# Four score and forget-gate matmuls per attention unit: two heads together, or head by head

## The chip, the cores and the metric

The kernel runs on one core of one Trainium2 chip. The metric is the device time of one execution in microseconds (us); lower is better. PE is TensorE, DVE is VectorE, ACT is ScalarE, POOL is GpSimd, SP issues the weight transfers. The kernel is written instruction by instruction: every engine has its own program, and semaphores tie the programs together.

## The reference

Two transformer blocks stand one behind the other, on 256 tokens of width 1024, all in float32. The change lies in the second block, in its forgetting attention (8 heads of width 64, computed in two query blocks of 128 tokens):

```python
q = rms_norm_2(heads(q), q_norm); k = rms_norm_2(heads(k), k_norm)      # B, H=8, S=256, hd=64
cum = jnp.cumsum(log_f, axis=-1)                                        # B, H, S
s = jnp.einsum('bhqd,bhkd->bhqk', q_i, k) * scale
s = s + c_i[..., :, None] - cum[..., None, :]                           # c_i: cum at the queries
s = jnp.where(pos_k[None, :] <= pos_q[:, None], s, -jnp.inf)
pr = jax.nn.softmax(s, axis=-1)
o = jnp.einsum('bhqk,bhkd->bhqd', pr, v)
```

Around it stand: rms norm and an input projection (w_in), an RWKV-7 mixer on the other half of the width, sigmoid gates, two projections (rwkv_proj, fox_proj), an output projection (w_out), and feed-forward parts before and after.

## The kernel before

All weights come in chunks of 1 MB (128 partitions x 2048 floats). SP loads a chunk into one of three `w_raw` buffers; ACT copies it to `w_hi` in the rounded format fp32r (L1316); DVE takes `w_lo` = `w_raw` - `w_hi` (L1602). PE multiplies in three parts, high x high, low x high, high x low (L1987, L1988, L1989): one chunk by columns is 48 matmuls of 128x256. PE's order is written out by hand, and so is that of ACT and DVE; nothing is scheduled by a planner.

The change is in `f_scores(it)`, a closure in `pe_mixer`. It computes the scores of one attention unit: `it` runs from 0 to 7, `t = it // 2` picks a pair of heads, `i = it % 2` the query block. With i = 0 the keys are 128 wide, with i = 1 they are 256 wide. The two heads of a pair lie in one tile of 128 partitions: head 0 in partitions 0 to 63, head 1 in partitions 64 to 127 (`head(v, h, ...)` takes that slice). So a score matmul contracts over 64 partitions. The forget term is added by a second matmul into the same bank: its left side is one column of the identity spread over 128 columns, its right side the cumulated forget gates, and both lie in partitions 32 to 39 (`32:32 + NH`, NH = 8), for either head. Head 0 goes to PSUM bank 4, head 1 to bank 5. These operands are plain float32, and the trace shows two matmul records for each such matmul of the program. The last of the four increments `f_scores`.

What follows a block: DVE adds the query's term and the causal mask (L1082) and takes the row maximum (L1088); ACT takes the exponential (L819); DVE normalizes (L1100); PE turns the probabilities (L695); ACT copies them out of PSUM (L830); PE multiplies by v (L706); ACT and DVE write the result as high and low part (L834, L1118).

The order on PE: block 0; the gate columns of chunk B_GA+3 with block 1 in their middle (after 18 of 48 matmuls); then for each unit `it`: a chunk of matmuls (gate columns for it < 5, a chunk of rwkv_proj by rows for it = 5 and 6), the transposes of unit `it`, `f_scores(it + 2)`, and the product with v of unit `it`. Blocks 2 to 7 so stand between L695 and L706. DVE's order in unit `it`: the gate columns out of PSUM (L1639), the scores of unit it+2, the normalization of unit it+1, the low part of the output of unit `it` (L1118), and the w_lo of a later chunk (L1602). The chunk of unit 5 waits until DVE has read the gate columns of unit 4 (L1639).

Of the kernel before, what the change touches and what calls it, by code (L numbers as in the profile page):

```python
# [14 lines left out]
P = 128  # L15
# [21 lines left out]
NH = HALF // HD  # L37
# [51 lines left out]
def block_pair(nc, inp, out, scratch, shifted):  # L89

    ctx = ExitStack()
    with ctx:
        S = Signals(nc, ctx)

        def sb(name, shape, dt=F32):
            return ctx.enter_context(nc.sbuf_tensor(name, shape, dt))

        bank = [ctx.enter_context(nc.psum_tensor(f"bank{b}", [P, 512], F32)) for b in range(8)]
# [7 lines left out]
        ident, ones, head_ones = sb("ident", [P, P]), sb("ones", [P, P]), sb("head_ones", [P, P])  # L106
# [7 lines left out]
        def region(at, *shape):  # L114
            n = int(np.prod(shape))
            assert at + n <= ARENA
            v = arena[:, at:at + n]
            if len(shape) == 2:
                v = v.rearrange("p (a b) -> p a b", a=shape[0])
            if len(shape) == 3:  # L120
                v = v.rearrange("p (a b c) -> p a b c", a=shape[0], b=shape[1])
            return v
# [210 lines left out]
        forget = region(18440, T)  # L333
# [6 lines left out]
        fq, fk = region(16384, HT, T), region(17408, HT, T)  # L340
# [92 lines left out]
        def head(v, h, *rest):  # L433
            return v[(slice(HD * h, HD * (h + 1)), *rest)]


        def pe_mixer(told, pe, state, by_columns, by_tokens, by_rows, rows_to_tokens, turn_late_half, spread):
# [42 lines left out]
            for t in range(HT):  # L480
                mm = pe.matmul(bank[6 + t // 2][:, t % 2 * T:t % 2 * T + T], lora_w[0:32, 0, t * P:(t + 1) * P],
                               lora_act[0:32, 0, :], start=True, stop=True)
            mm.then_inc(S["decay_in"], told.one("decay_in"))
            for t in range(HT):
                mm = pe.matmul(bank[4 + t // 2][:, t % 2 * T:t % 2 * T + T], lora_w[32:64, 0, t * P:(t + 1) * P],
                               lora_act[32:64, 0, :], start=True, stop=True)
# [7 lines left out]
            for t in range(HT):  # L494
                o = bank[6 + t // 2][:, t % 2 * T:t % 2 * T + T]
                pe.matmul(o, lora_w[64:128, 0, t * P:(t + 1) * P], lora_act[64:128, 0, :], start=True, stop=False)
                mm = pe.matmul(o, lora_w[0:32, 1, t * P:(t + 1) * P], lora_act[0:32, 1, :], start=False, stop=True)
# [8 lines left out]
            for tt in range(TT):  # L506
                mm = pe.matmul(bank[3][:, 256 + tt * NH:256 + (tt + 1) * NH], forget[32:32 + NH, tt * P:(tt + 1) * P],
                               ident[32:32 + NH, 32:32 + NH], start=True, stop=True)
# [5 lines left out]
            for t in range(HT):  # L514
                mm = pe.matmul(bank[6 + t // 2][:, t % 2 * T:t % 2 * T + T], head_ones[:, :], early[:, t, :],
                               start=True, stop=True)
# [5 lines left out]
            for c in range(NCH):  # L522
                if c > 1:
                    pe.wait_ge(S["masked"], 2 * (c - 1))
                for src, b in ((b_dec, 4 + 2 * (c % 2)), (k_dec, 5 + 2 * (c % 2))):
                    for t in range(HT):
                        for h in range(2):
                            mm = pe.matmul(head(bank[b], h, slice(t * P, (t + 1) * P)),  # L528
                                           head(src, h, t, slice(c * CHUNK, (c + 1) * CHUNK)),
                                           head(ar, h, c * HT + t), start=True, stop=True)  # L530
# [10 lines left out]
            for u in range(NCH * HT):  # L541
                for h in range(2):
                    mm = pe.matmul(head(bank[6 + u // 8], h, slice(u % 8 * CHUNK, u % 8 * CHUNK + CHUNK)),
                                   head(xt_inv, h, u), head(ident, h, slice(HD * h, HD * (h + 1))),
                                   start=True, stop=True)
# [54 lines left out]
            for c in range(NCH):  # L600
                def each(fn):
                    for t in range(HT):
                        for h in range(2):
                            mm = fn(t, h, c * HT + t)
                    return mm

                def cell(b, t, h):
                    return head(bank[b], h, slice(t * CHUNK, (t + 1) * CHUNK))

                def mul(o, left, right, start, stop):  # L610
                    return pe.matmul(o, left, right, start=start, stop=stop, skip_group_check=True)  # L611

                def decayed(k, u, h):
                    return head(ar, h, u, slice(k * CHUNK, (k + 1) * CHUNK))

                pe.wait_ge(S["xt_added"], 2 * LEVELS)
                if c > 0:
                    pe.wait_ge(S["w_copied"], c)
                mm = each(lambda t, h, u: mul(cell(4, t, h), head(m_k, h, u, slice(0, CHUNK)), head(v_tok, h, u),
                                              t == 0, not c and t == HT - 1))  # L620
                if c:
                    pe.wait_ge(S["state"], c)
                    mm = each(lambda t, h, u: mul(cell(4, t, h), decayed(0, u, h), head(state_t, h, t), False,
                                                  t == HT - 1))
# [22 lines left out]
            for t in range(HT):  # L647
                mm = pe.matmul(bank[4 + t // 2][:, t % 2 * T:t % 2 * T + T], head_ones[:, :], y_t[:, t, :],
                               start=True, stop=True)
# [13 lines left out]
            def f_scores(it):  # L663

                t, i = divmod(it, TT)
                w = P * (i + 1)
                if it == 0:
                    pe.wait_ge(S["normed_by_head"], 6)
                else:
                    pe.wait_ge(S["f_scores_read"], 2 * it)  # L670
                for h in range(2):

                    pe.matmul(bank[4 + h][:, 0:w], head(fq, h, t, slice(i * P, (i + 1) * P)),
                              head(fk, h, t, slice(0, w)), start=True, stop=False)
                for h in range(2):
                    c = 32 + 2 * t + h
                    mm = pe.matmul(bank[4 + h][:, 0:w], ident[32:32 + NH, c:c + 1].to_broadcast([NH, P]),
                                   forget[32:32 + NH, 0:w], start=False, stop=True)
                mm.then_inc(S["f_scores"], told.one("f_scores"))

            f_scores(0)
            for it in range(FUNITS):
                t, i = divmod(it, TT)
                if it < 5:
                    columns(B_GA + 3 + it, midway=(lambda: f_scores(1)) if it == 0 else None)
                elif it < 7:

                    r = it - 5
                    pe.wait_ge(S["y_lo"], 1)
                    for b, c in enumerate(all_read(B_RP)):  # L690
                        pe.wait_ge(S[f"bank{b}_read"], c)
                    by_rows(B_RP + r, (B_RP + r) % RING, 0, Y_hi, Y_lo, 2 * r, r == 0, r == 1)
                pe.wait_ge(S["f_probs"], it + 1)
                for b in range(2 * (i + 1)):
                    mm = pe.transpose(bank[6][:, b * P:(b + 1) * P], fs_t[:, it % 2, b * P:(b + 1) * P], ident[:])  # L695
                mm.then_inc(S["f_probs_turned"], told.one("f_probs_turned"))
                if it + 2 < FUNITS:
                    f_scores(it + 2)
                pe.wait_ge(S["fpT_ready"], it + 1)
                if it > 0:  # L700
                    pe.wait_ge(S["f_out_lo"], it)
                for h in range(2):
                    for kb in range(i + 1):
                        b = h * (i + 1) + kb
                        c = (2 * t + h) * HD
                        mm = pe.matmul(head(bank[7], h, slice(0, P)), fv[:, kb, c:c + HD],  # L706
                                       fpT[:, b * P:(b + 1) * P], start=kb == 0, stop=kb == i)
                mm.then_inc(S["f_pv_done"], told.one("f_pv_done"))
# [1568 lines left out]
```

## Time and profile before

| | |
|---|---|
| median of 3 runs | 1203.66 us (1203.29 to 1204.83) |
| profiled execution, its time | 1203.29 us |
| its span | 1201.5 us |
| PE busy | 1144.5 us, 95% |
| DVE busy | 771.0 us, 64% |
| ACT busy | 557.2 us, 46% |
| granted TensorE clock, mean | 0.981 |
| first and last score block (L673) | start 895.17 and 947.57 us |

The span runs from the first to the last instruction that the profile shows; the execution's time is 1.8 us longer. A matmul's record has a modelled end, and records overlap, so the cost of a group of matmuls is best read from its start to the start of what comes next. A merged row of the time order shows the start of the first record, the stretch that the group covers, and after it how many records there are. In brackets stands how long the engine had been idle, and what ended that.

### The profile page before, as it was taken

To read this page: it belongs to the slowest core of one execution; us is meant where nothing else is said; L and a number is where in the kernel's file an instruction comes from. 1 tells how busy PE (TensorE), PEld (TensorE's weight loads), DVE (VectorE), ACT (ScalarE), POOL (GpSimd) and SP (SyncE) were. 2 spreads that over 40 slices of the span, in tenths; PEclk is the share of its full clock that TensorE was granted. 3 is DMA by queue.
4 is the path that set the end of the run, shared out by engine and by line. 5 is a ranking of instruction groups with operands and counts; after the bars stand their busy time and mean duration, and the time that the engine had idled before them with its cause. 6 is when DMAs were issued, how large, how long until landed. Compare 5 with 4: busy or idle time off the path is not lost.

```text
span 1201.5 us, 22075 instructions
## 1 busy us (share of the span) xinstructions
PE 1144.5 (95%) x9584; PEld 1078.9 (90%) x9584; DVE 771.0 (64%) x1042; ACT 557.2 (46%) x660; POOL 150.0 (12%) x112
## 2 busy tenths in 40 slices
PE   7999999989999999899999979999899889999997
PEld 6999999988899999799999968989898778999996
DVE  4888976747686777756455656963257655645554
ACT  6333445473764455654433454422334446434433
POOL 5888760000000000000000000012000000000000
PEclk9999999999999999999999988999999989999999
DMA  8586553344365555555556524323033433565651
GB/s 255 179 290 199 176 175 106 116 161 173 109 208 193 183 201 175 174 175 166 185 176 208 184 97 140 106 75 104 3 106 105 141 106 124 193 213 188 201 163 56
DMA packets 144315, 188.94 MB, mean 157 GB/s; under 512 B 4448, under 2 KB 128921, under 8 KB 144237
## 3 DMA queue, kind: packets, MB, share of 16 engines
q1 hardware_dynamic: 142941, 184.28, 46.3%
q0 software_dynamic: 1104, 3.49, 0.9%
q8 instruction: 58, 0.95, 0.3%
q14 instruction: 20, 0.16, 0.0%
q10 hardware_dynamic: 192, 0.05, 0.0%
HBM read 186.74 MB, written 2.64 MB: 158 GB/s over the span
## 4 chain that ended last, share of the span: by engine, by line
PE 84%; DVE 8%; ACT 5%; issue 2%; ACTq 0%; POOL 0%; DVEq 0%; POOLq 0%
PE bank L1987 19%; PE bank L1988 19%; PE bank L1989 19%; PE bank L2097 5%; PE bank L2098 5%; PE bank L2099 5%; PE bank L551 2%; DVE w_lo L1602 2%; ACT w_hi L1316 2%; PE bank L611 1%; DVE bank L1819 1%; PE bank L2224 1%; ACT sq L1330 1%; DVE x L1676 1%; PE bank L528 1%
## 5 line engine op out<-in xcount | busy, mean ns | idle before, releaser
L1987 PE MATMUL bank<-X_hi,w_hi 128*128 128x256 f32 x1840 | 527.2, 287 | 3.3 <-DVE w_lo L1775 2.9
L1988 PE MATMUL bank<-X_lo,w_hi 128*128 128x256 f32 x1840 | 523.6, 285 | 0.0
L1989 PE MATMUL bank<-X_hi,w_lo 128*128 128x256 f32 x1840 | 523.5, 285 | 0.0
L1316 ACT ACTIVATE w_hi<-w_raw 128x2048 fp32r<-128x2048 f32 x171 | 326.2, 1909 | 176.1 <-PE bank L1989 134.3
L1602 DVE TENSOR_TENSOR w_lo<-w_raw,w_hi 128x2048 fp32r<-128x2048 f32 x146 | 333.7, 2286 | 84.3 <-ACT w_hi L1316 84.0
L1987 PEld LDWEIGHTS bank<-X_hi,w_hi 128*128 128x128 f32 x1840 | 356.1, 194 | 8.6 <-issue 6.8
L1988 PEld LDWEIGHTS bank<-X_lo,w_hi 128*128 128x128 f32 x1840 | 356.2, 194 | 1.2
L1989 PEld LDWEIGHTS bank<-X_hi,w_lo 128*128 128x128 f32 x1840 | 356.0, 193 | 0.0
L1714 DVE TENSOR_TENSOR arena<-bank,rstd 128x512 f32<-128x512 f32 x66 | 45.6, 691 | 185.1 <-PE bank L1989 179.6
L1268 POOL TENSOR_TENSOR w_lo<-w_raw,w_hi 128x2048 fp32r<-128x2048 f32 x24 | 111.3, 4646 | 32.5 <-ACT w_hi L1316 32.4
L2097 PE MATMUL bank<-w_hi,Y_hi 128*128 128x512 f32 x264 | 103.3, 391 | 1.2 <-DVE Y_lo L1742 1.2
L2098 PE MATMUL bank<-w_hi,Y_lo 128*128 128x512 f32 x264 | 103.1, 390 | 0.0
L2099 PE MATMUL bank<-w_lo,Y_hi 128*128 128x512 f32 x264 | 102.7, 389 | 0.0
L1819 DVE SCALAR_TENSOR_TENSOR bank<-arena,par,bank 128x256 f32<-128x256 f32 x232 | 93.2, 484 | 0.6
L1297 POOL TENSOR_TENSOR arena<-arena,levels 128x512 f32<-128x512 f32 x10 | 12.8, 1282 | 592.6 <-DVE arena L1012 559.2
L2097 PEld LDWEIGHTS bank<-w_hi,Y_hi 128*128 128x128 f32 x264 | 49.7, 188 | 11.1 <-DVE Y_lo L1742 1.6
L2099 PEld LDWEIGHTS bank<-w_lo,Y_hi 128*128 128x128 f32 x264 | 49.6, 188 | 10.6
L2098 PEld LDWEIGHTS bank<-w_hi,Y_lo 128*128 128x128 f32 x264 | 49.7, 188 | 9.1
L1427 ACT ACTIVATE arena<-arena,par 128x256 f32<-128x256 f32 x44 | 24.1, 595 | 69.5 <-DVE arena L1714 69.5
L1436 ACT ACTIVATE arena<-arena 128x512 f32<-128x512 f32 x22 | 13.9, 633 | 84.1 <-DVE arena L1714 84.1
L1639 DVE TENSOR_TENSOR arena<-bank,rstd 128x512 f32<-128x512 f32 x43 | 29.6, 689 | 31.9 <-PE bank L1989 29.4
L1450 ACT ACTIVATE Y_hi<-arena 128x512 fp32r<-128x512 f32 x33 | 20.9, 632 | 44.0 <-DVE arena L1735 44.0
(285 smaller groups left out, 1291.9 us busy)
## 6 DMA issues: line engine op xcount, KB each, us to landing
w_raw<-in_ffn_w_dram SPq DMA_DIRECT2D x66, 1024.0 KB, 5.2
w_raw<-in_w_in_dram SPq DMA_DIRECT2D x53, 1024.0 KB, 5.1
w_raw<-in_w_up_dram SPq DMA_DIRECT2D x22, 1024.0 KB, 5.0
w_raw<-in_w_down_dram SPq DMA_DIRECT2D x11, 1024.0 KB, 4.9
w_raw<-in_w_out_dram SPq DMA_DIRECT2D x8, 1024.0 KB, 4.8
w_raw<-in_conv_pw_w_dram SPq DMA_DIRECT2D x4, 1024.0 KB, 4.9
w_raw<-in_w_attn_out_dram SPq DMA_DIRECT2D x2, 1024.0 KB, 5.1
w_raw<-in_rwkv_proj_dram SPq DMA_DIRECT2D x2, 1024.0 KB, 4.9
```

The source lines that it names most:

```text
L1268: g.tensor_tensor(w_lo[n % RING][:, :], raw[n % RING][:, :], w_hi[n % RING][:, :].bitcast(F32), ALU.subtract).then_inc(S["w_lo_pool"], tol ...
L1316: a.activation(w_hi[slot][:, :], raw[slot][:, :], ACT.Copy).then_inc(S["w_hi"], told.one("w_hi"))
L1602: v.tensor_tensor(w_lo[slot][:, :], raw[slot][:, :], w_hi[slot][:, :].bitcast(F32), ALU.subtract).then_inc(S["w_lo"], told.one("w_lo"))
L1639: v.tensor_tensor(dst, pairs(b), over(rstd[:], 2), ALU.mult).then_inc(S[f"bank{b}_read"], 1)
L1714: v.tensor_tensor(u_t[:, side].rearrange("p (m t) -> p m t", m=2), pairs(2 * (i % 2) + side), over(rstd[:], 2), ALU.mult).then_inc(S[name] ...
L1819: v.scalar_tensor_tensor(out=conv[:, t, :] if k == CONV_W - 1 else part, in0=src, scalar=w, in1=part, op0=ALU.mult, op1=ALU.add).then_inc( ...
L1987: pe.matmul(o, wh, xh, start=start, stop=False, skip_group_check=True)
L1988: pe.matmul(o, wh, xl, start=False, stop=False, skip_group_check=True)
L1989: return pe.matmul(o, wl, xh, start=False, stop=stop, skip_group_check=True)
L2097: pe.matmul(o, yh, wh, start=first and k == 0, stop=False, skip_group_check=True)
L2098: pe.matmul(o, yl, wh, start=False, stop=False, skip_group_check=True)
L2099: mm = pe.matmul(o, yh, wl, start=False, stop=last, skip_group_check=True)
```

## The change

The loop over the two heads with the two score matmuls, and the second loop with the two forget matmuls, become one loop: score and forget of head 0, then score and forget of head 1. The matmuls themselves, their banks, their start and stop flags, the waits ahead of them and the one signal behind them are the same.

```diff
                 for h in range(2):
 
-                    pe.matmul(bank[4 + h][:, 0:w], head(fq, h, t, slice(i * P, (i + 1) * P)),
-                              head(fk, h, t, slice(0, w)), start=True, stop=False)
-                for h in range(2):
+                    o = bank[4 + h][:, 0:w]
                     c = 32 + 2 * t + h
-                    mm = pe.matmul(bank[4 + h][:, 0:w], ident[32:32 + NH, c:c + 1].to_broadcast([NH, P]),
-                                   forget[32:32 + NH, 0:w], start=False, stop=True)
+                    pe.matmul(o, head(fq, h, t, slice(i * P, (i + 1) * P)), head(fk, h, t, slice(0, w)),
+                              start=True, stop=False)
+                    mm = pe.matmul(o, ident[32:32 + NH, c:c + 1].to_broadcast([NH, P]), forget[32:32 + NH, 0:w],
+                                   start=False, stop=True)
                 mm.then_inc(S["f_scores"], told.one("f_scores"))
```

On PE, block 3 (256 keys wide), between the transposes of unit 1 and the product with v. L673 and L675 are the score matmul before and now, L677 the forget matmul; `arena` holds queries, keys and gates, `ident` the identity; the number behind `bank` is the PSUM bank:

```order
 L1989 MATMUL bank1<-X_hi,w_lo1 128x256
 L695 MATMUL bank6<-ident,arena 128x128 x4
-L673 MATMUL bank4<-arena 128x256
-L673 MATMUL bank5<-arena 128x256
+L675 MATMUL bank4<-arena 128x256
 L677 MATMUL bank4<-arena,ident 128x256
+L675 MATMUL bank5<-arena 128x256
 L677 MATMUL bank5<-arena,ident 128x256
 L706 MATMUL bank7<-arena 64x128 x4
```

The score of bank 5 moved behind the forget matmul of bank 4. Block 4 (128 keys wide), in the same place of unit 2:

```order
 L1989 MATMUL bank2<-X_hi,w_lo2 128x256
 L695 MATMUL bank6<-ident,arena 128x128 x2
-L673 MATMUL bank4<-arena 128x128
-L673 MATMUL bank5<-arena 128x128
+L675 MATMUL bank4<-arena 128x128
 L677 MATMUL bank4<-arena,ident 128x128
+L675 MATMUL bank5<-arena 128x128
 L677 MATMUL bank5<-arena,ident 128x128
 L706 MATMUL bank7<-arena 64x128 x2
```

The same move; all eight blocks have it. DVE, ACT, POOL and SP keep their order in every row.

## Rows read from the trace of the kernel before

**Rows 1.** The page: busy us (share of the span) xinstructions of each engine.
```profile
PE 1144.5 (95%) x9584; PEld 1078.9 (90%) x9584; DVE 771.0 (64%) x1042; ACT 557.2 (46%) x660; POOL 150.0 (12%) x112
```
**Rows 2.** PE in order of time, block 2: start us, us, engine line operation, rows*columns, records.
```profile
905.76 0.49 PE L673 MATMUL bank<-arena 64*128 64x128 f32 x4
906.18 0.71 PE L677 MATMUL bank<-arena,ident 8*128 8x128 f32 x4
906.82 0.44 PE L706 MATMUL bank<-arena 128*64 128x128 f32 x4
907.19 0.38 PE L1987 MATMUL bank<-X_hi,w_hi 128*128 128x256 f32 x1
```
**Rows 3.** PE in order of time, block 1 (256 keys).
```profile
900.07 0.70 PE L673 MATMUL bank<-arena 64*128 64x256 f32 x4
900.70 1.12 PE L677 MATMUL bank<-arena,ident 8*128 8x256 f32 x4
901.76 0.38 PE L1987 MATMUL bank<-X_hi,w_hi 128*128 128x256 f32 x1
```
**Rows 4.** PE in order of time, block 1, only records that lie in 900.07 to 900.30.
```profile
900.07 0.49 PE L673 MATMUL bank<-arena 64*128 64x256 f32 x2
```
**Rows 5.** PE in order of time, L496 (64 partitions) and L497 (32 partitions) by turns.
```profile
736.61 0.70 PE L496 MATMUL bank<-arena 64*128 64x256 f32 x2
737.23 0.69 PE L497 MATMUL bank<-arena 32*128 32x256 f32 x2
737.86 0.70 PE L496 MATMUL bank<-arena 64*128 64x256 f32 x2
...
739.93 1.22 PE L497 MATMUL bank<-arena 32*128 32x256 f32 x2
741.07 1.22 PE L496 MATMUL bank<-arena 64*128 64x256 f32 x2
```
**Rows 6.** PE groups by line and shape, 895 to 950: busy us, mean ns, idle before.
```profile
L673 PE MATMUL bank<-arena 64*128 64x256 f32 x16 | 2.8, 428 | 0.0
L673 PE MATMUL bank<-arena 64*128 64x128 f32 x16 | 2.0, 322 | 2.0 <-DVE arena L1066 2.0
```
**Rows 7.** PE in order of time, blocks 4 and 6 and what follows them.
```profile
922.45 0.71 PE L677 MATMUL bank<-arena,ident 8*128 8x128 f32 x4
923.66 0.44 PE L706 MATMUL bank<-arena 128*64 128x128 f32 x4 [0.50 <-ACT arena L830]
...
939.29 0.71 PE L677 MATMUL bank<-arena,ident 8*128 8x128 f32 x4
939.93 0.44 PE L706 MATMUL bank<-arena 128*64 128x128 f32 x4
941.22 0.36 PE L1987 MATMUL bank<-Y_hi,w_hi 128*128 128x256 f32 x1 [0.85 <-DVE w_lo L1602]
```
**Rows 8.** DVE in order of time, 906.9 to 950.
```profile
906.98 0.61 DVE L1082 SCALAR_TENSOR_TENSOR arena<-bank,small,causal 128x128 f32<-128x128 f32 x2 [0.19 <-DVE arena L1639]
...
910.96 2.29 DVE L1602 TENSOR_TENSOR w_lo<-w_raw,w_hi 128x2048 fp32r<-128x2048 f32 x1 [1.51 <-ACT w_hi L1316]
...
933.39 0.88 DVE L1082 SCALAR_TENSOR_TENSOR arena<-bank,small,causal 128x256 f32<-128x256 f32 x2
...
949.37 0.88 DVE L1082 SCALAR_TENSOR_TENSOR arena<-bank,small,causal 128x256 f32<-128x256 f32 x2 [2.06 <-PE bank L677]
```
**Rows 9.** Stretches: length, busy us (records) of PE PEld DVE ACT POOL, clock, DMA.
```profile
908.00:911.40 3.40, 3.40 (x31) 3.40 (x30) 1.54 (x5) 2.85 (x6) 0.00 (x0) 1.00 0.72 286
...
739.50:742.90 3.40, 3.40 (x8) 1.49 (x6) 3.23 (x8) 0.00 (x0) 0.00 (x0) 0.50 0.54 170
...
896.60:899.80 3.20, 3.20 (x17) 3.20 (x16) 0.83 (x3) 2.30 (x5) 0.00 (x0) 0.50 0.04 10
961.40:964.70 3.30, 2.98 (x14) 2.99 (x15) 1.00 (x4) 3.29 (x3) 0.00 (x0) 0.50 0.60 190
978.50:981.80 3.30, 3.30 (x8) 2.56 (x9) 2.19 (x2) 1.62 (x1) 0.00 (x0) 0.50 0.00 0
```

## The prediction, made before the changed kernel ran

> **What bounds the kernel now.** I read the page first. PE is busy for 95% of the span [rows 1], so anything that makes PE's own instruction stream longer counts, unless it falls into a time in which PE waits. Next I read PE in order of time around the score blocks, from start to start, because the modelled ends overlap. A block of 128 keys takes 0.42 us for the four score records and 0.64 us for the four forget records, 1.06 us together, to the start of L706 [rows 2]. A block of 256 keys takes 0.63 + 1.06 = 1.69 us [rows 3]. The reader is to see that equally many records of equal width take 0.63 us in the one line and 1.06 us in the other. The reason is in the narrower view: two score records together cover 0.49 us [rows 4], though such a record lasts 0.43 us in the mean [rows 6]; one behind the other they would cover twice that. The scores of the two heads lie in disjoint halves of the array's rows and run side by side. The forget matmuls use the same 8 partitions for both heads and run one behind the other.
>
> **Part 1: what the new order makes of a block.** The pair of scores is torn apart, and between any two matmuls the contraction now changes from 64 partitions to 8 or back. Before, it changed once within a block; now three times. The nearest rows are L496 and L497 of the same mixer, which alternate between 64 partitions (64 to 127) and 32 partitions (0 to 31), 256 wide, in plain float32 like these. There each matmul of the program (two records) takes 0.62 to 0.63 us from start to start: 736.61, 737.23, 737.86 [rows 5]. Although their rows are disjoint, nothing runs side by side.
>
> For 256 keys I take this price for each of four matmuls: 4 x 0.625 = 2.50 us, against 1.69 before: +0.81 us. A check from the block itself: the score pair takes 0.63 us as two that run together, so one alone takes 0.63 too. Two forget matmuls take 1.06 us; the second adds two records in a row, 0.43 us, so one alone takes 0.63.
>
> For 128 keys there is no alternating row. By the same reasoning one score alone is the 0.42 us of the pair [rows 2], and one forget matmul alone is 0.64 less two records in a row. Those are 0.43 / 2 = 0.215 us at 256 wide, so 0.107 at 128, and 0.64 - 2 x 0.107 = 0.42. Four of them: 1.68, against 1.06: +0.6 us. Both are estimates from these rows.
>
> The bounds of this unknown: at least nothing, if the forget matmul of head 0 and the score of head 1 (rows 32 to 39 and 64 to 127) hid each other wholly and cost no more than the torn pair gave; at most what I take, since L496 and L497 hide nothing at all. I take the upper value, as those rows are the same kind of change of shape.
>
> **Part 2: how many blocks, and what hides them.** There are 16 score records of each width between 895 and 950 [rows 6], four records to a block: four blocks of 128 (0, 2, 4, 6) and four of 256 (1, 3, 5, 7). All of it would be 4 x 0.6 + 4 x 0.81 = 5.6 us. Not all of it is on the path:
>
> - Blocks 0, 1 and 2 (895 to 907) stand in an unbroken PE stream: block 0 follows a wait of 2.0 us for DVE that ends only when its operands are there [rows 6], and after block 2 L706 starts without idle time [rows 2]. DVE reads the scores of block 2 at 906.98, 0.16 us after L706 started, and had nothing else to do [rows 8]. So 0.6 + 0.81 + 0.6 = 2.0 us go into the time, and DVE and ACT are pushed back by the same 2.0 us.
> - From there to 941 DVE and ACT have a chain of their own. DVE's idle times in this stretch end by ACT, as the 1.51 us ahead of L1602 [rows 8], and ACT's by DVE; when DVE comes to the scores of block 5 (933.39) it doesn't wait for PE. PE waits for this chain twice. After block 4, L706 starts 1.21 us after L677 instead of 0.64, so 0.57 us is a wait; before the chunk of unit 5, L1987 starts 1.29 us after L706 instead of 0.37 [rows 2, 7], so 0.92 us is a wait (the row names L1602, but DVE's next instruction, the L1639 that frees the bank, is what is awaited). Together 1.49 us. Blocks 3 to 6 lengthen PE's stream by 0.81 + 0.6 + 0.81 + 0.6 = 2.8 us against it; 1.3 us is left over. Behind that leftover the next late thing is PE itself, no longer the bank.
> - Block 7 (947.57): DVE had been idle for 2.06 us and waits for exactly this block [rows 8], and the end of the attention hangs on it. +0.81 us in full.
>
> Sum: 2.0 + 1.3 + 0.8 = +4.1 us. What comes after (projections, feed-forward) is fed by this chain and only shifts.
>
> **Part 3: nothing else moves.** The wait ahead of a block, the one signal behind it, DMAs and the order of the other four engines are the same. The transfers are issued behind w_lo, which gets no earlier; later chunks land with more lead, at no cost. Below nothing there would be a gain only if head 0's bank were read sooner, but the signal is still one, on the last matmul.
>
> Against its own time: 1203.29 (profiled execution, 1.8 us outside its span of 1201.5) + 4.1 = 1207.4. The median of the three runs is 0.37 us above that execution, so I predict 1207.8 us.
>
> **The rivals.**
> 1. *The forget matmul of head 0 and the score of head 1 run side by side.* For it: their rows are disjoint, and the two scores show that disjoint rows can share the array [rows 4]. Against it: L497 and L496 are disjoint too and do not [rows 5]. A block would be three matmuls long: 3 x 0.625 = 1.88 (+0.19) and 3 x 0.42 = 1.26 (+0.2). Blocks 0 to 2 give 0.6, blocks 3 to 6 give 0.8 and go into the 1.49 us of waits, block 7 gives 0.2: +0.8 us, 1204.5 us. A sentence of the Trainium skill speaks for it: "TensorE: Matmul & The Clock Gate", part 3, "The mechanism", has matmuls on different row groups overlap, weight loads included, whenever the groups differ. The page "TensorEngine Tiling (Array Packing)", "Key Properties", excludes the case in which the size of the tile changes, for which it says the engine has to drain first. The trace sides with the second page: 0.62 us for each by turns against 0.49 for two of one size.
> 2. *The clock falls after the longer blocks.* At half clock 17 records stand in 3.2 us, which makes 18 in 3.4, and at full clock 31 in 3.4 [rows 9]: 13 fewer, of 3.4 / 31 = 0.11 us each, so a stretch of that length costs 1.4 us. For it: during L496 and L497 the clock is at 0.50 (1.2 GHz) from 739.5 on [rows 9], and PE had not been idle ahead of it, it had only alternated; the next matmuls take 1.14 us each instead of 0.62 (739.93 to 741.07) [rows 5]. Against it: a block of 256 alternates for 2.5 us only and has full-size matmuls right before and behind it, while those had the two-column matmuls of `head_sums` ahead. One to four such stretches: +1.4 to +5.6, so 1209.2 to 1213.4 us.
> 3. *Not slower after all: half-clock stretches go away.* Three lie in reach, at 896.6, 961.4 and 978.5, all at 0.50 [rows 9]. The change moves everything behind it by 2 to 4 us, so a stretch could fall elsewhere. Each is worth 1.4 us, and it decides only if all three go: 4.2 us against 4.1, so 1203.6 us. Against it: each follows a wait of PE for DVE or ACT (the 2.0 us ahead of block 0 in [rows 6] is the first), and none of these waits gets shorter.
>
> **How the numbers follow.** Forecast 0.74, rival 1 0.10, rival 2 0.13, rival 3 0.03. The forecast's own range is 1206.3 to 1209.2: below, the leftover of the middle blocks is hidden wholly (2.0 + 0.8 = +2.8) and a run is at the low end of the three; above, all 5.6 us count. The range for 8 in 10 takes in rival 1 and rival 2 with its first stretch and some spread: 1204.4 to 1210.6. No change that can be told is within 0.2%, or 2.4 us: 1201.3 to 1206.1. Rival 1, most of rival 3 and the lower tail of the forecast lie there: 0.18. Faster by over 0.2% is left 0.02. Slower is 0.80: the rest of the forecast, and rival 2.
>
> **What would show each step.** PE in order of time: L675 and L677 by turns, two records each, 0.62 us apart at 256 and 0.42 at 128; a block of 256 about 2.5 us, one of 128 about 1.7. If L675 of head 1 starts with L677 of head 0, rival 1 holds. The wait of L706 behind block 4 and the wait ahead of unit 5's chunk are gone; the waits behind block 7 are as long as before. The stretch from the start of block 0 to the first matmul of fox_proj grows by 4.1 us, and nothing behind it grows. The prediction would be wrong if the middle blocks were hidden by more than 1.5 us, or if the row of half-clock stretches differs from before between 900 and 957.

## The result: slower, by more than was forecast

| | before | changed kernel |
|---|---|---|
| median beside it, 5 executions each | 1203.66 us (1203.25 to 1206.28) | 1215.77 us (1211.01 to 1218.58) |
| ratio, 95% interval | | 1.008 (1.0054 to 1.0105) |
| repeated later, medians (23 and 12 executions) | 1205.38 us | 1214.73 us, ratio 1.0063 (1.0040 to 1.0086) |
| profiled execution, time / span | 1203.29 / 1201.5 us | 1212.24 / 1210.5 us |
| mean granted TensorE clock in it | 0.981 | 0.977 |

The direction was forecast; the size was not. I predicted 1207.8 us with a range up to 1210.6, and the median lies 5 us above that range. With 89 executions of before at hand (1202.7 to 1213.9 us, mean 1206.7) and 42 of the changed kernel (1209.3 to 1218.9, mean 1213.9) the change costs 7.2 us in the mean. The forecast was 4.1, from a base that lay too low. (The 89 are those of later comparisons; the five of before in the table are not among them.)

**The profile after.** PE in order of time, block 1 (256 keys) and block 2 (128 keys); columns as in [rows 2]:

```profile
902.52 0.70 PE L675 MATMUL bank<-arena 64*128 64x256 f32 x2
903.14 0.69 PE L677 MATMUL bank<-arena,ident 8*128 8x256 f32 x2
903.77 0.70 PE L675 MATMUL bank<-arena 64*128 64x256 f32 x2
904.39 0.69 PE L677 MATMUL bank<-arena,ident 8*128 8x256 f32 x2
905.02 0.39 PE L1987 MATMUL bank<-X_hi,w_hi 128*128 128x256 f32 x1
...
910.51 0.49 PE L675 MATMUL bank<-arena 64*128 64x128 f32 x2
910.92 0.48 PE L677 MATMUL bank<-arena,ident 8*128 8x128 f32 x2
911.34 0.48 PE L675 MATMUL bank<-arena 64*128 64x128 f32 x2
911.75 0.48 PE L677 MATMUL bank<-arena,ident 8*128 8x128 f32 x2
912.16 0.44 PE L706 MATMUL bank<-arena 128*64 128x128 f32 x4
```

Each matmul stands alone: 0.62 us apart at 256 and 0.41 at 128. A block takes 2.50 and 1.65 us, against 1.69 [rows 3] and 1.06 [rows 2]. The score of head 1 does not start beside the forget matmul of head 0.

The two waits of [rows 7], behind block 4 and ahead of the chunk of unit 5, in the changed kernel:

```profile
929.41 0.48 PE L677 MATMUL bank<-arena,ident 8*128 8x128 f32 x2
929.83 0.44 PE L706 MATMUL bank<-arena 128*64 128x128 f32 x4
...
949.00 0.44 PE L706 MATMUL bank<-arena 128*64 128x128 f32 x4
949.37 0.39 PE L1987 MATMUL bank<-Y_hi,w_hi 128*128 128x256 f32 x1
```

Both are gone: 0.42 and 0.37 us from start to start, no idle time in brackets. The waits behind block 7 are as long as they were. First the changed kernel, then the same two rows of before:

```profile
968.66 0.66 PE L706 MATMUL bank<-arena 128*64 128x128 f32 x8 [1.77 <-ACT arena L830]
970.71 0.58 PE L1987 MATMUL bank<-Y_hi,w_hi 128*128 128x256 f32 x1 [1.38 <-DVE Y_lo L1118]
```

```profile
959.67 0.66 PE L706 MATMUL bank<-arena 128*64 128x128 f32 x8 [1.78 <-ACT arena L830]
961.72 0.58 PE L1987 MATMUL bank<-Y_hi,w_hi 128*128 128x256 f32 x1 [1.38 <-DVE Y_lo L1118]
```

From block 0 (895.17 and 897.02) to this L1987 it is 66.5 us before and 73.7 after: +7.1, not +4.1. From there to the last matmul it is 231.6 us in both. What is new within the stretch is the clock. Stretches of the changed kernel, columns as in [rows 9]:

```profile
905.60:909.00 3.40, 3.40 (x19) 3.40 (x18) 3.33 (x6) 1.09 (x4) 0.00 (x0) 0.50 0.00 0
...
936.30:939.70 3.40, 3.40 (x21) 1.73 (x19) 2.84 (x5) 0.60 (x1) 0.00 (x0) 1.00 0.49 131
939.70:943.10 3.40, 3.40 (x18) 3.40 (x17) 1.90 (x6) 2.22 (x6) 0.00 (x0) 0.50 0.45 182
```

Two stretches run at 0.50 (1.2 GHz) and have no counterpart before; a third, at 898.8, is that of before at 896.5, behind the wait ahead of block 0. One starts 0.6 us behind block 1 (ended 905.02), the other 0.6 us behind block 5 (ended 939.08). PE was never idle ahead of either. At 1.4 us each they are 2.8 of the 7.1 us; 4.3 us are left for the length, against 4.1 forecast.

Two more half-clock stretches have nothing to do with the change, since they lie hundreds of microseconds ahead of it. The same places, in before and then in the changed kernel:

```profile
282.00:292.00 10.00, 8.31 (x37) 6.88 (x38) 8.46 (x11) 4.93 (x6) 0.00 (x0) 1.00 0.58 199
503.00:513.00 10.00, 8.30 (x67) 7.62 (x66) 5.73 (x13) 7.04 (x20) 0.00 (x0) 1.00 0.18 71
```

```profile
282.00:292.00 10.00, 8.55 (x30) 6.88 (x31) 8.21 (x11) 4.92 (x6) 0.00 (x0) 0.83 0.59 195
503.00:513.00 10.00, 7.94 (x50) 7.20 (x51) 7.42 (x15) 6.31 (x18) 0.00 (x0) 0.83 0.35 133
```

The instructions there are the same, the granted clock differs. It goes the other way too: between 712 and 749 before has six such stretches and the changed kernel five. Such stretches come and go from one execution to the next, and with them most of the spread of one kernel's times over 10 us (the fit below).

### The profile page after: what moved, and what is told of

Read it like the earlier page. It is cut to its first block, busy times and chain, and to the rows that moved or that the text cites. A ratio compares the mean times of both kernels' runs of the same rounds, so it can differ in the third digit from the quotient of the medians.

```text
span 1210.5 us, 22075 instructions
## 1 busy us (share of the span) xinstructions
PE 1155.8 (95%) x9584; PEld 1086.6 (90%) x9584; DVE 770.4 (64%) x1042; ACT 557.2 (46%) x660; POOL 149.9 (12%) x112
## 4 chain that ended last, share of the span: by engine, by line
PE 87%; DVE 7%; ACT 4%; issue 2%; DMA 0%; ACTq 0%; DVEq 0%
PE bank L1987 20%; PE bank L1988 20%; PE bank L1989 19%; PE bank L2097 5%; PE bank L2098 5%; PE bank L2099 5%; PE bank L551 2%; DVE w_lo L1602 2%; ACT w_hi L1316 1%; PE bank L611 1%; PE bank L2042 1%; PE bank L2224 1%; DVE bank L1819 1%; PE bank L675 1%; PE bank L677 1%
## 5 line engine op out<-in xcount | busy, mean ns | idle before, releaser
L1987 PE MATMUL bank<-X_hi,w_hi 128*128 128x256 f32 x1840 | 529.2, 288 | 2.8 <-issue 2.7
L1987 PEld LDWEIGHTS bank<-X_hi,w_hi 128*128 128x128 f32 x1840 | 358.1, 195 | 8.0 <-issue 6.1
L1427 ACT ACTIVATE arena<-arena,par 128x256 f32<-128x256 f32 x44 | 24.1, 595 | 69.5 <-DVE arena L1714 69.5
```

The source lines that it names most:

```text
L1987: pe.matmul(o, wh, xh, start=start, stop=False, skip_group_check=True)
```

## How the experiments are read

Two measures separate length from clock. The first is the trace: the **attention stretch**, from block 0 to the first fox_proj matmul, less 1.4 us for each half-clock stretch in which PE works. Before it is 66.5 - 1.4 = 65.1 us. Where a pad stands ahead of block 0, the stretch starts with the pad. The second is over all executions. Every one lists its span and its mean granted clock, so the time at half clock is 2 x (1 - clock) x span. One line fitted to 243 executions of all kernels, with a constant for each kernel, has a slope of 0.40 us per us at half clock (3.4 us x 0.40 = 1.4 us again) and leaves 1.0 us of scatter. A kernel's constant less that of before is its **length**.

| kernel | median (n) | median of before | ratio, 95% interval | mean time at half clock | length | attention stretch |
|---|---|---|---|---|---|---|
| before | 1205.7 (89) | | | 50.5 ± 0.7 us | 0 | 65.1 |
| changed, all | 1214.3 (42) | | | 57.8 ± 1.0 | +4.3 ± 0.2 | 69.5, 69.6 |
| only 256 | 1208.19 (12) | 1205.34 | 1.0024 (1.0006 to 1.0042) | 51.3 ± 1.7 | +2.1 ± 0.3 | 67.1 |
| only 128 | 1209.85 (12) | 1205.34 | 1.0026 (1.0010 to 1.0042) | 53.1 ± 1.4 | +1.6 ± 0.3 | 66.4 |
| blocks 3 to 6 | 1208.99 (12) | 1206.40 | 1.0016 (0.9995 to 1.0036) | 52.5 ± 1.5 | +1.5 ± 0.3 | 66.5 |
| short full-array pad | 1211.19 (9) | 1205.34 | 1.0040 (1.0019 to 1.0060) | 52.9 ± 2.2 | +3.3 ± 0.4 | 68.3 |
| short 2-column pad | 1210.93 (11) | 1205.34 | 1.0043 (1.0022 to 1.0064) | 55.2 ± 2.1 | +1.9 ± 0.3 | 67.5 |
| long full-array pad | 1222.59 (4) | 1205.38 | 1.0129 (1.0083 to 1.0175) | 50.1 ± 1.8 | +16.1 ± 0.5 | 81.4 |
| long 2-column pad | 1242.74 (4) | 1205.38 | 1.0288 (1.0241 to 1.0335) | 96.2 ± 1.9 | +18.3 ± 0.7 | |
| gates paired | 1208.01 (12) | 1205.38 | 1.0001 (0.9977 to 1.0026) | 55.7 ± 1.6 | -1.3 ± 0.3 | 63.9 |
| paired in 0, 1, 2, 7 | 1205.77 (12) | 1206.40 | 0.9987 (0.9965 to 1.0009) | 49.8 ± 1.3 | +0.1 ± 0.3 | 63.8 |
| waits filled | 1202.64 (12) | 1206.40 | 0.9958 (0.9938 to 0.9979) | 40.2 ± 1.3 | +0.2 ± 0.3 | |
| filled, and paired in 0, 1, 2, 7 | 1200.95 (12) | 1206.40 | 0.9944 (0.9925 to 0.9964) | 38.4 ± 1.0 | -0.8 ± 0.3 | |

The ± are standard errors. For the changed kernel this gives 4.3 us of length and 7.3 us more at half clock, x 0.40 = 2.9 us: 7.2 together, the difference of the means.

## The experiments

**The changed kernel again.** No edit.

> The changed kernel once more, beside before on the same chip, since executions of before spread from 1202.7 to 1211.2 us when there are 31 of them. Theory C (4.1 us of length, and more time at half clock for the rest): its median is 7 to 9 us above that of before; the runs with the same granted clock differ by 4 to 5 us; in the trace the stretch from block 0 to the first fox_proj matmul, less 1.4 us for each half-clock stretch in it, is 4.1 us longer than before, and at least one half-clock stretch starts within 1 us behind a block of 256 keys. Theory L (length alone): at the same granted clock the runs differ by the whole 7 to 9 us.

Measured: 9.4 us above before by the medians (expected 7 to 9), length +4.3 with the earlier executions. The trace has three new half-clock stretches: one from 903.0, which joins on to the one behind the wait ahead of block 0, and those at 923.5 and 961.1. Stretches of this execution:

```profile
899.60:903.00 3.40, 3.40 (x14) 2.76 (x14) 1.03 (x3) 0.46 (x3) 0.00 (x0) 0.50 0.03 7
903.00:906.40 3.40, 3.40 (x14) 2.67 (x13) 0.00 (x0) 2.22 (x4) 0.00 (x0) 0.50 0.01 2
...
920.10:923.50 3.40, 3.40 (x19) 1.91 (x20) 3.33 (x7) 0.60 (x1) 0.00 (x0) 1.00 0.56 153
923.50:926.90 3.40, 3.40 (x20) 3.07 (x19) 3.29 (x7) 0.32 (x1) 0.00 (x0) 0.50 0.40 160
957.70:961.10 3.40, 3.40 (x20) 1.90 (x20) 0.84 (x2) 0.60 (x1) 0.00 (x0) 0.99 0.80 254
961.10:964.50 3.40, 3.40 (x19) 3.40 (x17) 1.51 (x5) 2.61 (x6) 0.00 (x0) 0.50 0.15 59
```

The full-clock stretches ahead of the last two hold block 3 and block 7, in order of time:

```profile
922.69 0.69 PE L677 MATMUL bank<-arena,ident 8*128 8x256 f32 x2
923.32 0.56 PE L706 MATMUL bank<-arena 128*64 128x128 f32 x4
...
959.52 0.69 PE L677 MATMUL bank<-arena,ident 8*128 8x256 f32 x2
960.15 0.66 PE L706 MATMUL bank<-arena 128*64 128x128 f32 x8
```

Over the two profiled executions a new half-clock stretch has followed each of the four blocks of 256 keys, but only two of them in each. These four start 0.2 to 1.0 us behind the block. The fifth, from 903.0, starts ahead of block 1 (905.40) and is no mark of the new order: the traces with long and short full-array pads have such a second stretch behind block 0 too (900.9 and 904.8), and there every block has the order of before.

**The new order in some of the blocks.** `order` holds (head, gate) pairs; the condition chooses the blocks. It is `i == 1` for only 256, `i == 0` for only 128 and `3 <= it <= 6` for blocks 3 to 6:

```diff
+                heads_apart = i == 1
+                order = [(0, 0), (0, 1), (1, 0), (1, 1)] if heads_apart else [(0, 0), (1, 0), (0, 1), (1, 1)]
...
```

> The new order only in the four blocks of 256 keys (1, 3, 5, 7). Length by the sum: 0.81 (block 1) + 0.13 (blocks 3 and 5, 1.62 less the 1.49 us of waits) + 0.81 (block 7) = 1.8 us. Theory C: these blocks alternate for 2.5 us, so most of the half-clock stretches come from them: 1206 to 1213 us. Theory L: the extra of the new order goes by length, of which these have 3.2 of 5.6 us: 1209 to 1211 us, without more half-clock stretches.

> The new order only in the four blocks of 128 keys (0, 2, 4, 6). Length by the sum: 0.6 + 0.6 (blocks 0 and 2) and 1.2 us of blocks 4 and 6 that the waits hide: +1.2, 1204.9 us. Theory C: hardly more half-clock stretches, since such a block is 1.7 us long: 1204.5 to 1206.5 us. Theory L: 2.4 of 5.6 us of length: 1208 to 1209 us.

> The new order only in blocks 3 to 6, which lie beside the chain of DVE and ACT. By the sum of the prediction: 2.8 us of PE's stream, 1.5 of it in place of waits, so +1.3 us of length (in the trace: the stretch from block 0 to fox_proj less 1.4 us for each half-clock stretch in it). If nothing there is hidden: +2.8. If all of it is hidden: 0. Theory C adds half-clock stretches: one on average, so the median is 2 to 4 us above before.

Measured lengths, by the executions and by the trace: +2.1 and +2.0 (expected 1.8), +1.6 and +1.2 (1.2), +1.5 and +1.3 (1.3). The last one is the step of which I was least sure: 2.8 us of PE's stream were added and 1.3 to 1.5 of them arrived, so the waits did absorb the rest. Nowhere does length cost much more than the sum said, and theory L falls. The median that I expected of the 128-key order, 1204.5 to 1206.5 us, was missed (1209.85): it stood on a base of 1203.66, where before had 1205.34 here, and on no clock for these blocks. What the means don't tell is which blocks bring the clock down: at half clock they spend 51.3, 53.1 and 52.5 us, within 2.6 us of before at errors of 1.4 to 1.7. That also speaks against the blocks of 256 keys as the whole cause: alone they have 6.5 us less at half clock than the changed kernel, at an error of 2.0.

The traces say where such stretches start. That of blocks 3 to 6 has one new, 0.2 us behind block 3 (ended 915.96), again with PE busy ahead of it:

```profile
912.80:916.20 3.40, 3.40 (x19) 1.90 (x19) 3.33 (x7) 0.60 (x1) 0.00 (x0) 0.99 0.58 161
916.20:919.60 3.40, 3.40 (x21) 3.07 (x18) 3.30 (x7) 0.38 (x1) 0.00 (x0) 0.50 0.38 152
```

That of only 256 is at 0.50 from 899.3 to 909.5, three stretches in a row; the last starts at 906.1, just behind block 1. So of the 11 blocks 1, 3 and 5 with the new order in four traces, five are followed within 1 us by the start of a half-clock stretch. In the nine traces that have these blocks in the order of before (that of the long 2-column pads left out), none of 27 is. Behind blocks 2, 4 and 6 with the new order none of 11 is. Block 7 is left out of the count, since PE's waits stand close behind it, and block 0, since one stands ahead of it.

**Short pads.** Ahead of each block's scores, into the bank that they overwrite; first the full-array pad, then the one of 2 columns:

```diff
+                pe.matmul(bank[4][:, 0:T], ident[:], ones[:, 0:1].to_broadcast([P, T]), start=True, stop=True)
+                if i:
+                    pe.matmul(bank[4][:, 0:P], ident[:], ones[:, :], start=True, stop=True)
```

```diff
+                for _ in range(3 if i else 2):
+                    pe.matmul(bank[4][:, 0:2], ident[:], ones[:, 0:2], start=True, stop=True)
```

> The order of before, and ahead of the scores of each block an extra plain float32 matmul on the full array (256 columns; in the blocks of 256 keys one of 128 columns more) into the bank that the scores then overwrite. So each block gets longer by about what the new order adds (0.6 and 0.8 us), with the array in full use. Theory C (the new order costs its length, 4.1 us, and beyond it half-clock stretches that follow the badly used array): about 1207.8 us, no half-clock stretch between 900 and 957 that isn't in the trace of before, and the runs lie close together. Theory L (the length alone costs 10 to 12 us, because less of it is hidden than I reckoned): the same time as the new order, 1212 to 1216 us.

> The order of before, and ahead of the scores of each block two (128 keys) or three (256 keys) plain float32 matmuls of only 2 columns. PE's stream gets longer by about the same 0.6 and 0.8 us, but the array hardly works in it. Theory C: like the new order, 1210 to 1218 us, with one to three more half-clock stretches between 900 and 965. Theory L: also 1212 to 1216, but with no more half-clock stretches than with the full-array matmuls. Against the run with full-array matmuls theory C expects 3 us or more, theory L nothing.

A miss for theory C as I had put it: 3 us were expected between the two, and the medians differ by 0.3; that of the full-array pads, 1211.19, lies 3.4 us above the 1207.8 expected. The full-array pads added 0.43 and 0.65 us instead of 0.6 and 0.8, two and three records in a row at 0.215 us and nothing extra for the change of tile size behind them. Those of 2 columns added 0.34 and 0.57 us, little beside what the new order does to a block. The means at half clock (52.9 and 55.2, errors of 2.1 to 2.2) can't be told apart. The traces went against theory C as well: the full-array pad has a new half-clock stretch after 900 (from 904.8, right behind the one at block 0), the pad of 2 columns has none that before has not. Inconclusive, so I made the dose larger.

**Long pads.** The same place, five matmuls of 256 columns, as here, or ten of 2 columns:

```diff
+                for _ in range(5):
+                    pe.matmul(bank[4][:, 0:T], ident[:], ones[:, 0:1].to_broadcast([P, T]), start=True, stop=True)
```

> The twin: instead of the ten small matmuls five plain float32 matmuls of 256 columns on the full array, 2.15 us. Both theories: about 16 us more than before (8 x 2.15 less the 1.5 us of waits), 1220 to 1222 us. Theory C: no half-clock stretch in the attention beyond those of before.

> The order of before, and ahead of the scores of each of the 8 blocks ten plain float32 matmuls of 2 columns, 2.2 us of PE's stream in which the array hardly works. Theory C: with the block behind them (1.1 to 1.7 us) they make a stretch that brings the clock down at nearly each block: four to eight half-clock stretches in the attention, mean granted clock below that of the run with full columns by 0.004 or more, and 4 us or more longer than that run. Theory L: same time as that run within 2 us.

One pad of each in order of time, first full columns, then 2 columns:

```profile
922.63 2.34 PE L672 MATMUL bank<-ones,ident 128*128 128x256 f32 x10
924.90 0.70 PE L675 MATMUL bank<-arena 64*128 64x256 f32 x4
```

```profile
920.34 2.31 PE L672 MATMUL bank<-ones,ident 128*128 128x2 f32 x20
922.58 0.80 PE L675 MATMUL bank<-arena 64*128 64x128 f32 x4
```

At full clock both hold PE for 2.2 to 2.3 us to the first score, and PE is busy without a gap in both. Stretches behind such pads, full columns first:

```profile
924.00:930.80 6.80, 6.80 (x51) 5.51 (x50) 5.14 (x9) 2.31 (x6) 0.00 (x0) 1.00 0.36 142
935.00:941.80 6.80, 6.80 (x55) 6.05 (x54) 3.17 (x7) 2.85 (x6) 0.00 (x0) 1.00 0.45 154
945.00:951.80 6.80, 6.80 (x52) 5.57 (x51) 2.35 (x6) 2.80 (x6) 0.00 (x0) 1.00 0.33 134
```

```profile
922.50:929.30 6.80, 6.80 (x34) 6.01 (x34) 2.81 (x7) 2.84 (x6) 0.00 (x0) 0.50 0.10 38
936.10:942.90 6.80, 6.80 (x32) 5.63 (x30) 2.35 (x6) 3.06 (x7) 0.00 (x0) 0.50 0.00 0
949.80:956.60 6.80, 6.80 (x34) 6.25 (x33) 4.14 (x7) 2.84 (x6) 0.00 (x0) 0.50 0.00 2
```

51 to 55 matmul records against 32 to 34 in the same 6.8 us. The one kernel spends 50.1 us at half clock, as before does, the other 96.2; the medians are 20.2 us apart for a PE stream that is nearly equally long at full clock. 46.1 us x 0.40 = 18 us of that is the half clock; the other 2 us are not accounted for. Theory C had the direction and not the size: it expected four to eight half-clock stretches in the attention and 4 us or more, and the trace has sixteen of 3.4 us between 902 and 994. The full-array pad has one in the attention that before has not, from 900.9, right behind the one at block 0. So the clock can fall while PE is busy without a gap, when its matmuls are only 2 columns wide.

**Gates paired.** A copy of the cumulated gates in partitions 96 to 103; all else as in before:

```diff
+            v.tensor_copy(forget[96:96 + NH, :], forget[rows_f, :]).then_inc(S["dve_step"], told.one("dve_step"))
+            dve.wait_ge(S["dve_step"], told.value("dve_step"))
...
-                    c = 32 + 2 * t + h
-                    mm = pe.matmul(bank[4 + h][:, 0:w], ident[32:32 + NH, c:c + 1].to_broadcast([NH, P]),
-                                   forget[32:32 + NH, 0:w], start=False, stop=True)
+                    r = 32 + HD * h
+                    c = r + 2 * t + h
+                    mm = pe.matmul(bank[4 + h][:, 0:w], ident[r:r + NH, c:c + 1].to_broadcast([NH, P]),
+                                   forget[r:r + NH, 0:w], start=False, stop=True)
```

> The order of before, but head 1's forget matmul reads a copy of the cumulated gates in partitions 96 to 103 (one small DVE copy), so that the two forget matmuls lie on disjoint rows like the two scores. If disjoint rows with the same tile size run side by side, two forget matmuls take 0.42 us (128 keys) and 0.63 (256) instead of 0.64 and 1.06, a block 0.84 and 1.26 us. Blocks 0 to 2 give 0.9 us back, blocks 3 to 6 nothing (PE only waits longer for DVE and ACT), block 7 0.4: 1.3 us faster than before. If forget matmuls don't pair whatever their rows are, the same time as before, and my account of why the scores pair is wrong.

Block 3 in order of time (L678 is the forget matmul here):

```profile
915.89 0.70 PE L673 MATMUL bank<-arena 64*128 64x256 f32 x4
916.53 0.70 PE L678 MATMUL bank<-arena,ident 8*128 8x256 f32 x4
917.16 0.66 PE L707 MATMUL bank<-arena 128*64 128x128 f32 x8
```

The forget matmuls now take 0.63 us for both, a block 1.27 (1.26 expected), and the length is -1.3 over the executions and -1.2 in the trace. Disjoint rows run side by side if the tile size is the same; that is the account of the pair in one experiment. But the 1.3 us that were expected did not come: the ratio to before is 1.0001. The mean at half clock went up from 50.5 to 55.7 us, x 0.40 = 2.1 us, more than the length gave. The wait ahead of unit 5's chunk is longer:

```profile
943.61 0.55 PE L1990 MATMUL bank<-Y_hi,w_hi 128*128 128x256 f32 x1 [1.50 <-DVE w_lo L1605]
```

1.50 us instead of 0.85 [rows 7], and a half-clock stretch starts at 943.4. That longer waits are why the mean rose fits this, but it was seen in one trace only.

**Paired only where PE is on the path.** `r = 32 + HD * h if it in (0, 1, 2, 7) else 32`.

> The paired forget matmuls (head 1 reads the copy in partitions 96 to 103) only in blocks 0, 1, 2 and 7, where PE's time is on the path; blocks 3 to 6 as before. Length as with all eight paired: 1.3 us less than before. Theory C: PE's waits in blocks 3 to 6 are longer than before by 0.9 us (the chain is earlier by that) but shorter than with all eight paired, so fewer half-clock stretches than there: median 1204 to 1206 us, 1 to 2 us faster than all eight paired.

The median is as expected, 2.2 us below all eight paired, and the mean at half clock is back at 49.8 us. The two measures of length disagree (-1.3 in the trace, +0.1 over the executions), so I claim no gain over before from it: the interval of the ratio contains 1.

**The waits filled.** `keep_busy(b, n)` issues n matmuls of 256 columns on the full array into bank b, whose contents are no longer or not yet needed:

```diff
+            keep_busy(6, 4)
             f_scores(0)
...
+                if it == FUNITS - 1:
+                    keep_busy(5, 3)
                 pe.wait_ge(S["fpT_ready"], it + 1)
...
+            keep_busy(5, 2)
             for n in range(B_FP, ffn_at[2]):
...
+                    if r == 0:
+                        pe.wait_ge(S["mixed"], 5)
+                        keep_busy(0, 4)
                     pe.wait_ge(S["mixed_lo"], 4 + r + 1)
```

> The order of before, and full-array matmuls of 256 columns (results unused) where PE waits for DVE and ACT: four ahead of block 0, three behind the last transposes, two ahead of fox_proj, four ahead of the last projection. They fill waits and should lengthen nothing. Theory C: half-clock stretches that follow these waits (896.5, 961.3 and 978.4 in before) go, 1.4 us each: 2.5 to 4 us faster than before, at a mean granted clock that is higher by 0.003 to 0.004. Theory L: no change, or slower.

> Both: the waits filled with full-array matmuls as in that kernel, and the forget matmuls of all eight blocks paired. Theory C: 1.3 us of length less, and the half-clock stretches at the waits gone: 3.5 to 5.5 us faster than before, the fastest version here.

The wait ahead of block 0 in order of time (L666 is the filler, L678 the score matmul here), and the clock behind the three places:

```profile
897.80 1.91 PE L666 MATMUL bank<-ones,ident 128*128 128x256 f32 x8
899.92 0.49 PE L678 MATMUL bank<-arena 64*128 64x128 f32 x4 [0.21 <-DVE arena L1078]
```

```profile
898.10:901.50 3.40, 3.19 (x20) 2.40 (x19) 2.01 (x6) 0.00 (x0) 0.00 (x0) 1.00 0.69 242
962.00:965.40 3.40, 2.93 (x20) 2.22 (x21) 1.79 (x2) 2.63 (x4) 0.00 (x0) 1.00 0.93 308
979.80:983.20 3.40, 3.40 (x14) 2.67 (x15) 2.53 (x4) 2.71 (x3) 0.00 (x0) 1.00 0.50 176
```

All three stretches that ran at 0.50 in before [rows 9] are at full clock. One trace alone would not show that the fillers did it (the trace of paired in 0, 1, 2, 7 has none behind block 0 either, without a filler), but twelve executions do: thirteen matmuls whose results nobody reads make the kernel 0.42% faster (0.21 to 0.62%), at no length, with 10 us less at half clock. This trace has one half-clock stretch in the attention, at 944.6, 0.1 us after the wait of 0.85 us ahead of unit 5's chunk, which was not filled.

The other kernel is not what its expectation says. Its edit has `r = 32 + HD * h if it in (0, 1, 2, 7) else 32`, so it pairs the forget matmuls in four blocks and not in all eight. It is 0.56% faster than before (0.36 to 0.75%), the fastest kernel here, with 38.4 us at half clock. The same four blocks cost no clock without the fillers either (49.8 us); whether eight paired blocks would cost none once the waits are filled was not run.

## Why the prediction was wrong

**What bounds the kernel, and part 1: right.** The price of a torn pair, from L496 and L497 at 256 and by subtraction at 128, was met: 2.50 us against 2.50 forecast, and 1.65 against 1.68. Rival 1, the score of head 1 beside the forget matmul of head 0, is out. By the rule of the Trainium skill that a change of tiling mode drains the engine ("TensorEngine Tiling (Array Packing)", "Key Properties"), the trace agrees, at 0.62 us for each of four matmuls; the paired gates agree from the other side, as 0.63 us for two.

**Part 2: right.** The sum gave +4.1 us. Over 131 executions of the two kernels the length is +4.3 ± 0.2; the traces give 4.3 and 4.4. Blocks 3 to 6 alone gave 1.3 to 1.5 where 1.3 was expected, both waits of PE vanished, and those behind block 7 kept their length.

**Rival 2: the step that failed.** The sum had no term for the clock. Rival 2 was given 0.13 and put beside the forecast as an alternative, priced at 1.4 us for each half-clock stretch. The price held (0.40 us per us). The chance did not: the mean over executions is 7.3 us more at half clock, about two stretches of 3.4 us in each, 2.9 us of time. I argued against it that a block of 256 alternates for only 2.5 us and has full-size matmuls on both sides. Four of the five new stretches in the two traces start right behind such blocks, with full-size matmuls on both sides. It should have been a term of the sum, which measured 2.9 us, since the trace of before had the alternation of L496 and L497 end at half clock [rows 5, 9] without any wait.

**The base: wrong too.** I added the change to a median of three executions as if their spread, 1.5 us, were the kernel's. Of 89, the median is 1205.7 and the mean 1206.7; 3 us of the miss against 1207.8 come from there. The one of the three whose clock is on record has 45.7 us at half clock, against 50.5 in the mean. In mean values: 1206.7 + 4.3 + 2.9 = 1213.9, which is the mean of the 42. The first five of the changed kernel lay 1.9 us above that by their median. That is luck of the draw in both kernels, and it makes the first comparison (12.1 us) larger than the change costs (7.2 us).

**Rival 3 did not happen:** there is more time at half clock, not less. That such stretches can be avoided is shown by another edit: with the waits filled the kernel has 10 us less of them and is 3.8 us faster by the medians.

**What stays open.** That the new order brings the clock down is shown by 42 against 89 executions and by where the new stretches start; that matmuls of 2 columns do so without a gap on PE, by the long pads. That it is the few rows of the alternating matmuls (64 and 8) is an inference from both; no run varied the rows alone. Which blocks do it, and whether 128-key blocks contribute, is not settled: by their means the partial orders differ from before by less than twice their errors, and the blocks of 256 alone fall short of the whole change. The short pads did not separate.

## What to carry to other kernels

Matmuls on disjoint rows of the array ran side by side here only next to one another and only at the same tile size (64 with 64 rows, 8 with 8, but neither 64 with 8 nor 64 with 32); before interleaving small matmuls by what they compute, look in the trace at whether two records of one line cover the time of one. A stretch in which PE is always busy can still cost clock, if its matmuls have few columns and, as the new order suggests, few rows. A wait of PE can be worth filling with matmuls whose results nobody reads. Where the clock comes and goes, compare kernels at equal granted clock over ten or more executions, and take no base from three.

## What the hardware showed beyond that

- Two kernels with the same instructions otherwise and 2.2 us of PE work at full clock added to each of eight blocks differ by 20 us: ten matmuls of 2 columns against five of 256. Where such a pad of 2 columns itself fell at half clock, it took 4.2 us (907.01 to 911.20, block 1).
- The time at half clock varies in one and the same kernel by 20 us and more between executions (mean granted clock 0.972 to 0.983 in before), and each us of it costs 0.40 us.
- Eight paired blocks are 1.3 us shorter in length and no faster, with 5 us more at half clock. That the longer waits of PE bring the clock down there fits one trace, and four paired blocks have no more than before.
